# Modulation sums by stage 2, 5, 1, 4, 5, 1 in place of 2, 5, 2, 5, 3, 1

## What is computed

```python
cs = jax.nn.silu(c)
for layer in range(DEPTH):                       # DEPTH = 2
    mod = (cs @ mod_w[layer] + mod_b[layer]).reshape(bsz, N_SUB, 3, D_MODEL)
    x = adaln_sublayer(x, mod[:, 0], <feed-forward>, ...)
    ...                                          # sublayers 1 and 2 with mod[:, 1], mod[:, 2]

def adaln_sublayer(x, m, f, ln_g, ln_b):
    shift, scale, gate = m[:, None, 0], m[:, None, 1], m[:, None, 2]
    y = f(x * (1 + scale) + shift)
    return layer_norm(DEEPNORM_ALPHA * x + (1 + gate) * y, ln_g, ln_b)
```

## Time and profile before

| what | value |
|---|---|
| median of 3 runs | 1729.71 us (1729.4 to 1730.54) |
| the profiled execution: its time, its span | 1730.29 us, 1728.5 us |
| PE busy (matmul) | 1512.7 us, 88% of the span |
| DVE busy | 1165.0 us, 67% |
| ACT busy | 867.9 us, 50% |
| chain that ended last | PE 75%, DVE 14%, ACT 6%, issue 2% |
| modulation tiles | 72 DMAs of 1 MB; DVE L354 126 instructions, L351 18 |

### The profile page before, as it was taken

One profiled execution on the slowest core, in us unless ns is written; L12 is line 12 of the kernel. 1 busy time (PEld: TensorE's weight loads), 2 busy tenths in 40 slices (PEclk: granted clock), 3 DMA queues, 4 the chain that ended last, 5 costly groups with the idle time before them and its releaser, 6 DMA issues.

```text
span 1728.5 us, 23733 instructions
## 1 busy us (share of the span) xinstructions
PE 1512.7 (88%) x8963; PEld 1303.5 (75%) x8963; DVE 1165.0 (67%) x2082; ACT 867.9 (50%) x1601; POOL 0.2 (0%) x4
## 2 busy tenths in 40 slices
PE   2999989867978999979999568799996998799987
PEld 2788879766856888868887567678885996589855
DVE  5888879738656888888866554587667454464364
ACT  0545544442164455455554446555455874485463
POOL 0000000000000000000000000000000000000000
PEclk8999989987878999989999789999997999998999
DMA  9898858720003898768864060266555450436100
GB/s 365 291 331 300 302 171 303 245 73 1 1 28 120 306 326 280 267 207 316 297 214 124 26 232 19 97 218 221 187 189 160 154 181 20 146 100 197 48 1 25
DMA packets 198413, 306.50 MB, mean 177 GB/s; under 512 B 11458, under 2 KB 160028, under 8 KB 198300
## 3 DMA queue, kind: packets, MB, share of 16 engines
q1 hardware_dynamic: 195472, 302.51, 51.5%
q10 hardware_dynamic: 2828, 2.48, 0.4%
HBM read 303.91 MB, written 1.05 MB: 176 GB/s over the span
## 4 chain that ended last, share of the span: by engine, by line
PE 75%; DVE 14%; ACT 6%; issue 2%; ACTq 1%; PEld 1%; PEldq 0%; DVEq 0%
PE bank L852 18%; PE bank L779 12%; PE bank L781 11%; PE bank L780 11%; PE bank L851 8%; PE bank L1302 3%; PE bank L1289 2%; PE bank L1319 2%; DVE zT L354 2%; DVE wp_lo L1087 1%; PE bank L854 1%; PE bank L372 1%; DVE w_lo L902 1%; ACT arena L1354 1%; DVE uT L573 1%
## 5 line engine op out<-in xcount | busy, mean ns | idle before, releaser
L852 PE MATMUL bank<-u_hi_lo,w_hi 128*128 128x512 f32 x1408 | 500.9, 400 | 11.5 <-DVE u_hi_lo L448 8.6
L851 PE MATMUL bank<-u_hi_lo,w_lo 128*128 128x256 f32 x1232 | 348.2, 283 | 1.0 <-DVE u_hi_lo L448 1.0
L902 DVE TENSOR_TENSOR w_lo<-weight_ring,w_hi 128x1024 fp32r<-128x1024 f32 x264 | 307.8, 1219 | 14.5 <-ACT w_hi L872 14.0
L852 PEld LDWEIGHTS bank<-u_hi_lo,w_hi 128*128 128x128 f32 x1408 | 261.2, 190 | 65.0 <-issue 9.8
L872 ACT CAST w_hi<-weight_ring 128x1024 fp32r<-128x1024 f32 x264 | 260.1, 1046 | 24.8 <-DMA weight_ring<-in_ffn_w_gate_dram 15.9
L851 PEld LDWEIGHTS bank<-u_hi_lo,w_lo 128*128 128x128 f32 x1232 | 235.0, 191 | 14.2 <-DVE u_hi_lo L448 6.3
L1087 DVE TENSOR_TENSOR wp_lo<-weight_ring,wp_hi 128x1024 fp32r<-128x1024 f32 (+4 forms) x149 | 167.4, 1163 | 45.0 <-ACT wp_hi L1054 44.8
L779 PE MATMUL bank<-src_hi,wp_hi 128*128 128x256 f32 (+1 forms) x632 | 188.9, 299 | 5.1 <-DVE src_lo L448 5.1
L780 PE MATMUL bank<-src_lo,wp_hi 128*128 128x256 f32 (+1 forms) x632 | 182.0, 288 | 0.0
L781 PE MATMUL bank<-src_hi,wp_lo 128*128 128x256 f32 (+1 forms) x632 | 181.8, 288 | 0.0
L1054 ACT CAST wp_hi<-weight_ring 128x1024 fp32r<-128x1024 f32 (+4 forms) x149 | 143.4, 1007 | 66.9 <-PE bank L781 50.1
(11 more groups left out here) (336 smaller groups left out, 2245.4 us busy)
## 6 DMA issues: line engine op xcount, KB each, us to landing
weight_ring<-in_mod_w_dram SPq DMA_DIRECT2D x72, 1024.0 KB, 6.9
weight_ring<-in_ffn_w_gate_dram SPq DMA_DIRECT2D x44, 1024.0 KB, 6.1
weight_ring<-in_ffn_w_up_dram SPq DMA_DIRECT2D x44, 1024.0 KB, 5.4
weight_ring<-in_ffn_w_down_dram SPq DMA_DIRECT2D x44, 1024.0 KB, 8.1
weight_ring<-in_hyb_w_in_dram SPq DMA_DIRECT2D x16, 1024.0 KB, 9.9
weight_ring<-in_w_in_e_dram SPq DMA_DIRECT2D x16, 1024.0 KB, 5.5
weight_ring<-in_w_in_o_dram SPq DMA_DIRECT2D x13, 1024.0 KB, 5.4
weight_ring<-in_hyb_w_out_dram SPq DMA_DIRECT2D x4, 1024.0 KB, 4.8
```

The costliest lines, as they stand in the source:

```text
L851: nc.tensor.matmul(bank[:, 0:SEQ], w[1], u[:, 0:SEQ], start=False, stop=False, skip_group_check=True)
L852: last = nc.tensor.matmul(bank[:, :], w[0], u, start=kt == 0, stop=kt == KT - 1, skip_group_check=True)
L902: nc.vector.tensor_tensor(part_view(wl, n, part), raw, part_view(wh, n, part).bitcast(F32), ALU.subtract).then_inc(w_lo.sem, w_lo.up())
```

## The change

One unit less is done behind the hybrid's projections (8 alone moves out), stage 3 does one unit less, stage 4 two more. Unit 8, the gate of sublayer 2, goes from the hybrid to the start of stage 3; units 12 and 13, shift and scale of sublayer 4, go from the end of stage 3 to the start of stage 4. `head_sum` waits for eight units taken instead of nine. The number of units, of tiles and of bytes is the same.

```diff
             def head_sum(pe, t):
 
                 pe.wait_ge(squared.sem, squared.base + t + 1)
-                pe.wait_ge(mod_taken.sem, 9)
+                pe.wait_ge(mod_taken.sem, 8)
...
-            projections(jobs, uT, post=post, slots=4, n_units=2, head=head, x_rows_of=(0, 3), pe_pre=pe_pre,
+            projections(jobs, uT, post=post, slots=4, n_units=1, head=head, x_rows_of=(0, 3), pe_pre=pe_pre,
                         act_mid=act_mid, dve_at=dve_at)
...
                  lambda: hybrid(LayerNorm(0)),
-                 lambda: ffn(2, 5, LayerNorm(1)),
-                 lambda: ffn(3, 3, LayerNorm(2)),
+                 lambda: ffn(2, 4, LayerNorm(1)),
+                 lambda: ffn(3, 5, LayerNorm(2)),
```

## The result

The changed kernel takes 1713.16 us (median of 4 runs, 1712.75 to 1713.82) against 1729.67 (4 runs, 1729.4 to 1730.54): a ratio of 0.9899, 95% interval 0.9887 to 0.991. The prediction is wrong in size, not in sign.

A forecast was written before the change was run, and what follows sets the result against it. PE was taken to set the pace near the edits, except at one hole in the hybrid where DVE's queue decides. Terms -9.44 - 1.99 + 3.79 = -7.64 us gave 1722.1 us from the median 1729.71; range 1720.4 to 1725.0.

The forecast's parts named there:

- What bounds the kernel, and the hole: Hybrid's projections, ahead of job 8: PE waits for DVE's unit 8; moving the unit out saves 9.44 us.
- DVE's hand count and SP's queue: Hybrid's jobs 6 to 11: job 8's low parts ready at 301.1, 2.1 us early; weight tiles cause no wait.
- A: Hybrid, job 8: low parts come on their old date, 2.0 us of idling remain; 1724.1 us, chance 0.09.
- B: Hybrid, job 8 or later: all 5.54 us of idling return as a wait for low parts; 1727.6 us, chance 0.07.
- The rule on the most-contended engine: Hybrid's hole: read as counting only the reduction's slow clock, not idle time; B's rule, 1727.6 us, chance 0.07.
- The clock: Reduction of unit 8 in the hybrid: about 2.06 of the 9.44 us is slow clock; nothing beyond to gain.
- Stages 3 and 4: Stage 3 loses a reduction and a late taking, -1.99 us; stage 4 gains two reductions and a taking, +3.79.
- a sign of being wrong: Stage 4: the prediction counts as wrong if this stage grows by more than 4 us.
- Rival C: Stage 4, steps 12 to 19: weight stream falls behind, two added reductions wait at slow clock, +15.2; 1737.3 us, chance 0.04.

The follow-up runs named there:

- the kernel with the hybrid's edit alone: Changed kernel with one unit moved back from stage 4 to stage 3 (units 5, 1, 5, 4, 1); 1714.35 us, ratio 0.993 to the kernel before.
- The experiment with the later reduction: Kernel before with unit 8 reduced ahead of job 9 instead of job 8, all sums staying in the hybrid; 1727.78 us, ratio 0.9985.
- the kernel with stages 3 and 4 alone: Kernel before with two units moved from stage 3 to stage 4, hybrid untouched (units 5, 2, 3, 5, 1); 1728.42 us, ratio 0.9993.

## Why the prediction was wrong

**What bounds the kernel, and the hole.** Right. 5.54 us of idling, 3.78 of reduction and a tenth: 9.44 forecast, 9.46 measured, and 9.26 in the kernel with the hybrid's edit alone (head to L1738: 106.29 us against 115.55).

**DVE's hand count and SP's queue.** Right, to 0.2 us. Rivals A and B, a wait in the place of the one removed, did not occur in the change. The experiment with the later reduction shows that A's 2.2 us are real where the unit stays: the room comes only from taking DVE's work away.

**The rule on the most-contended engine** (the Trainium skill, "Perfetto Trace Analysis", section "Identifying the Most-Contended Engine"). The prediction read it as if idle time did not count, 1727.6 us. The page doesn't say that: right behind the rule, in "Optimization Strategy", it has one find the gaps on that engine and what blocks it, which leads to this very hole. The trace agrees: PE, busy 88% of the span, stood 5.54 us for DVE, and with the unit gone 9.46 us came back. So this rival was built on a wrong reading of the rule.

**The clock.** The step counted 2.06 us of the reduction as clock and said that nothing beyond job 8 was to be gained. That was the failure, together with the next sentence, "the 9.44 us should arrive at the end of the stage whole". The 9.44 us did arrive at the end of the projections; but from there to stage 3's head the hybrid gained another 7.78, a term that the sum put at nothing. It took the clock of the stretches behind the edit for a property of their work. The trace of before held the warning: in the recurrence PE fell from 2.4 to 1.2 GHz inside work with no idle gap over 1.33 us, and such a fall may go the other way when everything is shifted. Its price could have been worked out from the rounds at either level (0.71 us for four of L2159's matmuls, then 1.22), and there was no rival for it; it is 6.7 us, 22.9 against 16.2. With it the forecast would have had a second value, 1722.1 - 6.7 = 1715.4, and a range down to 1720.4 - 6.7 = 1713.7. The measured 1713.16 lies half a microsecond lower still, by the parts in the other stretches.

**Stages 3 and 4.** Right on what was counted: -1.93 against -1.99, and a unit at 1.81 in the kernel with four in stage 4. Stage 4 grew by 4.67 instead of 3.79, which the prediction had named as a sign of being wrong (more than 4 us). The 0.88 too much lie in its first 22 us, ahead of any modulation sum's end: from L573 to the first Silu of the stage 22.40 us against 21.48, with the clock falling and rising at other points of it. The 25 us behind the start of the products, in the kernel before and in the changed one:

```profile
755.00:780.00 25.00, 23.98 (x115) 19.34 (x114) 21.41 (x29) 13.67 (x21) 0.00 (x0) 0.90 0.85 293
```

```profile
736.60:761.60 25.00, 23.44 (x111) 18.87 (x110) 20.49 (x28) 13.65 (x21) 0.00 (x0) 0.86 0.51 173
```

The clock is 0.90 and 0.86, with 115 matmuls done in the one and 111 in the other. The same stage with the same five units took 208.67 us in the kernel with stages 3 and 4 alone. So this too fits the clock and not the units. And stage 5 gave 2.17 us back behind it; in seven of the eight traces with four and five units in stages 3 and 4 the two together take 376.5 us, however they share it. Rival C did not occur.

**The range and the runs.** The range was built from bounds of the structure, 0.3 us below the forecast and 2.3 above, and a margin for a spread of half a microsecond, taken from three runs that happened to agree. The 70 runs of the kernel before spread over 13 us. Four runs of the changed kernel all fell into its lower group, the other five split two to three. So a median of few runs can give anything between some 11 us (1731 against 1720) and 17.5 (1731.5 against 1714). That the changed kernel's runs near 1720 are those with the slow recurrence is an inference from the 6 us between its groups; no trace of one was taken. And their distance from the bulk of the kernel before, 11 us and not 7.6, says that further stretches, such as `mla`, differ too; how they share it is open. That the first four fell together was luck, and so was the agreement of the three before them.

## What to carry to other kernels

Where a profile has stretches of small dependent matmuls, read the granted clock of each and write down what each would take at the other level: a change ahead of them can flip them, as here 1.72 us did, and that price belongs in the range. Look also at where the clock last rose ahead of such a stretch: here some 0.1 us of distance to it parted the fast traces from the slow ones. Before a change of half a per cent is believed, shift the kernel by a microsecond or two of useless work and see whether the gain stays; where the runs of one kernel spread over 10 us, four runs of each settle little. An idle gap of PE ahead of a latency-bound stretch can be worth filling with useless matmuls, if the filling fits into the gap; here it gave 1.1 us.

## What the runs showed of the hardware

In the recurrence of the kernel before PE's clock fell from 2.4 to 1.2 GHz though PE had been busy for 8.67 of the 10 us before, with gaps of at most 1.33 us:

```profile
449.66:459.66 10.00, 8.67 (x71) 7.87 (x70) 6.47 (x16) 3.51 (x9) 0.00 (x0) 1.00 0.00 0
```

In the kernels with a fast recurrence it stayed up through the same work. The Trainium skill, "TensorE: Matmul & The Clock Gate", section "HAM oscillation — how this bites in real kernels", puts the fall to the slow clock down to long waits between bursts of matmuls; in the recurrence it fell without such a wait. The section that follows it there, "A second HAM failure mode: psum-queue depth-cycling", has short and frequent idling between groups of matmuls as a second cause, and that is nearer to the gaps of 0.5 and 1.33 us seen here. The same program gave times 13 us apart (0.75%), and adding 1.72 us of work made the kernel before 5.6 us faster in the median.
